# Order of softmax and splits in the pair units, forget gates moved to a value unit, gating and two token sums moved to GpSimd

## The chip, the cores and the metric

One NeuronCore of one Trainium2 chip. The kernel is one launch. Its time is the device time of the execution in microseconds, as the median of several runs. The engines are TensorE (PE in the rows, its weight loads PEld), VectorE (DVE), ScalarE (ACT), GpSimd (POOL) and SyncE (SP), which only issues DMAs here. Each engine runs its own list of instructions in order, and they wait for one another by semaphores. ScalarE and VectorE read the accumulators of TensorE (PSUM banks `acc` 0 to 3 and `side` 0 to 3); GpSimd works on SBUF alone.

## The reference

Two blocks on 512 tokens of 1024 features, all in float32. The first (gated pooling and a chunkwise linear recurrence) is over before the stretch that is touched. The second is a layer with four branches:

```python
def hybrid_layer(x, norm_g, w_in, ...):
    h = rms_norm_2(x, norm_g)
    (a_u, a_v, a_z, b_q, b_c, b_qi, b_ki, b_wi, b_z,
     c_b, c_c, c_x, c_z, d_q, d_k, d_v, d_f, d_z, gates) = split(h @ w_in)
    y_a = chunked_spatial_gating(a_u, a_v, ...) * silu(a_z)
    y_b = dsa_attention(b_q, b_c, b_qi, b_ki, b_wi, ...) * silu(b_z)
    y_c = short_gated_conv(c_b, c_c, c_x, conv_w) * silu(c_z)
    y_d = forgetting_attention(d_q, d_k, d_v, d_f, b_f) * silu(d_z)
    g = sigmoid(gates.reshape(b, s, 4, 1024))
    merged = sum_n g[n] * (y_n @ w_branch[n])
    return x + merged @ w_out

def forgetting_attention(q, k, v, f_logit, b_f):      # 4 heads of 128
    cum = cumsum(log_sigmoid(f_logit + b_f), axis=1)
    logits = q k^T / sqrt(128) + cum_q - cum_k        # causal
    return softmax(logits) v
```

## The kernel before

**Units.** The weights stream through as units of 128x1024 (some narrower), in the order `USED`. Each matrix product runs as three products of float32r parts: the weight is split into an upper part `w_hi` on ScalarE (`split_hi`, L713) and a lower part `w_lo` on VectorE (`split_lo`, L1308), and the tokens lie as `hT_hi` and `hT_lo`. Splits run ahead of their use. SyncE fetches the strips into a ring of five, GpSimd issues the DMAs that add up weights in DRAM for the pairs.

**The stretch.** After the units of branches a and c come four value units `dv` 0 to 3 (512 tokens, four accumulator banks, copied out to `fox_v` when `dv` 3 is done: two tiles by ScalarE, two by VectorE), then eight pairs `pa`, `pb`, `pd`, `pc` (p = 0 to 7), then `ga` 0, `ga` 1, `br` 0, `ga` 2, `ga` 3, `br` 1, and from there pairs of gates with `sa`, `sb`, `br`, `sc`, `sd`. A pair makes two panels (of q, k and the gates z of branches b and d) with seven instead of eight quarter products each (Strassen). For that, sums and differences of token quarters are made: tokens 1 and 2, 5 and 6 (`t_full` 5 and 6, for the `pc` units) and 4 and 3 (for `sc` and the third product of `br`). Each has an upper part `t_hi` (ScalarE) and a lower part `t_lo` (VectorE). The counter `t_step` follows the order in which they are made.

**A pair on the engines.** TensorE runs `pa` (one quarter product, twelve products of 128x256), `pb` (two), the slot of `pb`, `pd` (one), `pc`'s first product, the first of the next pair (`quad_first`), the slot of `pc`, `pc`'s second product. ScalarE copies four first parts (`keep_first` L927, L966, L974, L986), VectorE adds the others to them (L1699). A bank is free again when its part is copied or added. From pair 4 on the panels are gates: ScalarE makes exp, VectorE a bound, ScalarE ln and exp (together the sigmoid, `gate_sigmoid`), and VectorE multiplies it to z (`quad_finish`); for gates 0 to 3 it also multiplies the result with branch b's output (`y_tmp`, L1528), ScalarE makes the upper part (`end_upper`) and VectorE the lower part (`end_lower`).

**Slots.** The attention scores of branches b (scores 0 to 15) and d (16 to 31) run between the units, in slots of which each has its list of scores: 12 to 15 in the slots of `dv` and the one before, 16 to 31 two by two in the slots of `pb` and `pc` of pairs 4 to 7. A score is product, maximum (VectorE), exp (ScalarE), scale (VectorE), transpose (TensorE, next slot, L2312), copy `probsT` (ScalarE, L829), product with the values (slot after, L2327). The transposes share one bank (`side` 2): each waits for the copy of the one before (`bank2_read`). On ScalarE and VectorE a unit first works off its own part and its splits, then the slot.

**Forget gates.** In slot `FORGET_AT` = 34 (`pb` 1) TensorE transposes the logits, and VectorE and ScalarE make the cumulated log of the sigmoid in turns (L1672 to L1691, L915 to L918). `CUM_AT` = 36 turns it back.

**The end.** In `br` 0 VectorE makes the four products and lower parts of branch d (`end_tile`), then multiplies the result banks of `br` 0 with the sigmoids (L1972), which frees them for `br` 1. In `ga` 2 and `ga` 3 it makes tokens 3 and 4 (L1313 to L1315, L1342 to L1344, L1351). GpSimd has no arithmetic in the whole stretch: it parks `y` of branch a in DRAM at about 597 us, and fetches it back when `pc` 7 is done (819.5 us).

Of the kernel before, what the change touches and what calls it, by code (L numbers as in the profile page):

```python
# [46 lines left out]
for j in range(2 * KT):  # L47
# [12 lines left out]
                                               (5, "lo"), (6, "lo"), (3, "full"), (4, "full"), (4, "lo"), (3, "lo")])}  # L60
# [60 lines left out]
def to_split(k):  # L121

    if USED[k][0] in QUAD:
        return {"pa": [k + 3, k + 4], "pc": [k + 2, k + 3]}.get(USED[k][0], [])
# [66 lines left out]
FORGET_AT, CUM_AT = 34, 36  # L191
# [65 lines left out]
def program(nc, dram, out):  # L257
    f32, f32r, bf16, i32 = mybir.dt.float32, mybir.dt.float32r, mybir.dt.bfloat16, mybir.dt.int32
    ALU, ACT, AX = mybir.AluOpType, mybir.ActivationFunctionType, mybir.AxisListType
    with ExitStack() as ctx:  # L260
# [129 lines left out]
        forget = at("forget", M + 24576, [4, 2, S])  # L390
# [205 lines left out]
        def _(pool):  # L596
# [100 lines left out]
        def _(act):  # L697
# [254 lines left out]
            def quad_unit(k, kind, p):  # L952

                ends = p - QUADS // 2
                if kind == "pa":
# [16 lines left out]
                if kind == "pc":  # L972
# [3 lines left out]
                    for later_k in to_split(k):  # L976
                        split_hi(later_k)
# [3 lines left out]
            def quad_end(k, p):  # L981

                if p + 1 < QUADS:
                    keep_first(p + 1)
                act.wait_ge(unit_used, k + 1)
# [8 lines left out]
            for k, (kind, j) in enumerate(USED):  # L994
                if kind in QUAD:
                    quad_unit(k, kind, j)
                    if k in SLOT_AT:
                        side_slot(SLOT_AT[k])
                        act_forget(SLOT_AT[k])
                    if kind == "pc":  # L1000
                        quad_end(k, j)
# [153 lines left out]
                n = {("av", 1): 1, ("av", 2): 2, ("dv", 1): 5, ("dv", 2): 6}.get((kind, j))  # L1155
# [5 lines left out]
                if (kind, j) == ("ga", 3):  # L1161
# [54 lines left out]
        def _(dve):  # L1216
# [100 lines left out]
            def make_tokens(kind, j):  # L1317
# [12 lines left out]
                for n in {("av", 2): (1,), ("au", 2): (2,), ("dv", 2): (5, 6)}.get((kind, j), ()):  # L1330
                    dve.wait_ge(t_step, T_STEP[n if n > 2 else 2, "full"])
                    dve.wait_ge(t_hi_made, T_HI[n])
                    nc.vector.tensor_tensor(out=t_lo[n][:, :, :], in0=full[n], in1=t_hi[n][:, :, :].bitcast(f32),
                                            op=ALU.subtract).then_inc(t_step, 1)
                n = {("dv", 0): 5, ("ga", 2): 4}.get((kind, j))
                if (kind, j) == ("ga", 2):
                    difference(t3_full[:, :, :], t3_part[:, :, :], hi[1, 1], lo[1, 1], hi[0, 1], lo[0, 1])
                if n is not None:
                    dve.wait_ge(t_step, T_STEP[2, "lo"])
                    if n == 5:  # L1340
                        dve.wait_ge(parked, 32)
                    then(nc.vector.tensor_tensor(out=full[n], in0=hi[1, 0], in1=t_hi[2][:, :, :].bitcast(f32), op=ALU.add))  # L1342
                    then(nc.vector.tensor_tensor(out=rest[n], in0=lo[1, 0], in1=t_lo[2][:, :, :].bitcast(f32), op=ALU.add))
# [1328 lines left out]
```

## Time and profile before

| what | value |
| --- | --- |
| timed runs | 1129.44 us median of 3 (1127.44 to 1131.29) |
| profiled execution | 1130.89 us, span 1129.1 us, mean granted clock 0.994 |
| TensorE busy | 1101.7 us (98%) |
| VectorE busy | 744.8 us (66%) |
| ScalarE busy | 530.4 us (47%) |
| GpSimd busy | 74.4 us (7%) |
| `dv` 0 to the end of `dv` 3's slot | 665.8 to 696.5 us |
| pairs | 696.5 to 819.1 us |
| `ga` 0 to `sd` 2 | 819.1 to 877.2 us |

Times in rows are microseconds from the start of the span. A row of a timeline is start, length, engine, line, operation, what is written from what, and, in brackets, how long the engine had been idle before it and what ended that. The granted clock is a share of full speed: 1.00 is 2.4 GHz, 0.50 is 1.2 GHz.

### The profile page before, as it was taken

Reading aid. Unit: us, or ns where it says so; the run is one execution under the profiler, and the core shown is the slowest. Engines: PE = TensorE matmul, PEld = TensorE weight load, DVE = VectorE, ACT = ScalarE, POOL = GpSimd, SP = SyncE. Lnnn points to the kernel's source line nnn. Section 1 sums busy time; section 2 is a strip of 40 time slices with the busy share of each in tenths; the row PEclk is TensorE's granted clock in tenths of the full one; section 3 lists DMA queues with packets and bytes.
Section 4 is the critical chain, followed back from the end, with each engine's and each line's share of the span. In section 5 each row is a group of like instructions: output and inputs, shape, how many; then the busy total and the mean of one; then the engine's idle time right before and its main releaser. Section 6 shows DMA issues by size and latency. Waiting matters only on the chain.

```text
span 1129.1 us, 18866 instructions
## 1 busy us (share of the span) xinstructions
PE 1101.7 (98%) x7632; PEld 945.6 (84%) x7632; DVE 744.8 (66%) x1195; ACT 530.4 (47%) x897; POOL 74.4 (7%) x110
## 2 busy tenths in 40 slices
PE   9999999999999999999999999898898999999997
PEld 8888888788888888877888878897787999999986
DVE  6875776854785246478789886667738655556653
ACT  7562353324674325534442343456663444344543
POOL 1010101111110101011110000000000000000000
PEclk9999999999999999999999999899999999999999
DMA  9688878978778724368777222453333545455541
GB/s 370 217 274 250 205 204 260 246 201 218 191 150 212 249 92 165 134 171 221 167 208 205 72 84 83 124 166 103 101 135 92 166 138 162 140 161 167 143 167 75
DMA packets 61302, 194.56 MB, mean 172 GB/s; under 512 B 5648, under 2 KB 5648, under 8 KB 60704
## 3 DMA queue, kind: packets, MB, share of 16 engines
q1 hardware_dynamic: 39824, 127.19, 33.5%
q0 software_dynamic: 21248, 66.13, 24.7%
q8 instruction: 61, 1.00, 0.3%
q14 instruction: 25, 0.20, 0.1%
q10 hardware_dynamic: 144, 0.03, 0.0%
HBM read 187.04 MB, written 58.20 MB: 217 GB/s over the span
## 4 chain that ended last, share of the span: by engine, by line
PE 45%; DVE 5%; ACT 3%; issue 2%; ACTq 0%; DVEq 0%
PE acc L2045 6%; PE acc L2047 6%; PE acc L2046 6%; PE acc L2053 4%; PE acc L2055 4%; PE acc L2057 4%; PE side L2053 2%; PE side L2057 2%; PE side L2055 2%; PE side L2046 2%; PE side L2045 2%; PE side L2047 2%; PE side L2327 1%; PE side L2343 1%; PE side L2312 1%
## 5 line engine op out<-in xcount | busy, mean ns | idle before, releaser
L1308 DVE TENSOR_TENSOR w_lo<-raw,w_hi 128x1024 fp32r<-128x1024 f32 (+2 forms) x224 | 257.3, 1154 | 191.3 <-ACT w_hi L713 189.9
L713 ACT ACTIVATE w_hi<-raw 128x1024 fp32r<-128x1024 f32 (+2 forms) x224 | 222.3, 998 | 122.5 <-PE acc L2047 80.1
L2045 PE MATMUL acc<-hT_hi,w_hi 128*128 128x512 f32 x520 | 207.2, 398 | 0.0
L2047 PE MATMUL acc<-hT_hi,w_lo 128*128 128x512 f32 x520 | 202.8, 390 | 0.0
L2046 PE MATMUL acc<-hT_lo,w_hi 128*128 128x512 f32 x520 | 202.6, 390 | 0.0
L2045 PEld LDWEIGHTS acc<-hT_hi,w_hi 128*128 128x128 f32 x520 | 97.7, 188 | 21.2 <-issue 1.6
L2047 PEld LDWEIGHTS acc<-hT_hi,w_lo 128*128 128x128 f32 x520 | 97.6, 188 | 20.8
L2046 PEld LDWEIGHTS acc<-hT_lo,w_hi 128*128 128x128 f32 x520 | 97.8, 188 | 18.9
L2053 PE MATMUL acc<-t_hi,w_hi 128*128 128x256 f32 x212 | 61.8, 291 | 3.9 <-ACT fox_q L974 3.9
L2045 PE MATMUL acc<-w_hi,hT_hi 128*128 128x512 f32 (+1 forms) x152 | 61.1, 402 | 1.3 <-DVE y_tmp L1469 0.8
L2055 PE MATMUL acc<-t_lo,w_hi 128*128 128x256 f32 x212 | 61.1, 288 | 0.0
L2057 PE MATMUL acc<-t_hi,w_lo 128*128 128x256 f32 x212 | 61.0, 288 | 0.0
L2053 PE MATMUL acc<-hT_hi,w_hi 128*128 128x256 f32 x208 | 60.0, 288 | 0.0
L2057 PE MATMUL acc<-hT_hi,w_lo 128*128 128x256 f32 x208 | 59.3, 285 | 0.0
L2055 PE MATMUL acc<-hT_lo,w_hi 128*128 128x256 f32 x208 | 59.3, 285 | 0.0
L2047 PE MATMUL acc<-w_hi,hT_lo 128*128 128x512 f32 (+1 forms) x152 | 58.8, 387 | 0.0
L2046 PE MATMUL acc<-w_lo,hT_hi 128*128 128x512 f32 (+1 forms) x152 | 58.7, 386 | 0.0
L2053 PEld LDWEIGHTS acc<-t_hi,w_hi 128*128 128x128 f32 x212 | 42.0, 198 | 4.4 <-ACT fox_q L974 4.1
L2055 PEld LDWEIGHTS acc<-t_lo,w_hi 128*128 128x128 f32 x212 | 41.9, 198 | 0.3
L2057 PEld LDWEIGHTS acc<-t_hi,w_lo 128*128 128x128 f32 x212 | 41.8, 197 | 0.0
L2053 PEld LDWEIGHTS acc<-hT_hi,w_hi 128*128 128x128 f32 x208 | 40.4, 194 | 0.3
L2055 PEld LDWEIGHTS acc<-hT_lo,w_hi 128*128 128x128 f32 x208 | 40.4, 194 | 0.3
(484 smaller groups left out, 2343.3 us busy)
## 6 DMA issues: line engine op xcount, KB each, us to landing
raw<-sums_kept SPq DMA_DIRECT2D x44, 512.0 KB, 3.6
sums_kept<-in_st POOLq DMA_DIRECT2D x11, 1536.0 KB
sums_kept<-in_st POOLq DMA_DIRECT2D x11, 1024.0 KB
sums_kept<-in_st POOLq DMA_DIRECT2D x22, 512.0 KB
sums_kept<-sums_kept POOLq DMA_DIRECT2D x22, 512.0 KB
raw<-in_st SPq DMA_DIRECT2D x22, 512.0 KB, 3.9
ada_raw<-in_ada SPq DMA_DIRECT2D x16, 512.0 KB, 11.5
raw<-in_wo SPq DMA_DIRECT2D x16, 512.0 KB, 5.7
```

The costliest lines, as they stand in the source:

```text
L713: nc.scalar.activation(split_at(k)[0][:, 0:WIDTH.get(kind, U)], strip_of(k), ACT.Copy).then_inc(hi_made, 1)
L1308: nc.vector.tensor_tensor(out=lo[:, 0:width], in0=strip_of(k), in1=hi[:, 0:width].bitcast(f32), op=ALU.subtract).then_inc(lo_made, 1)
L2045: nc.tensor.matmul(ps, w[0], x[0], start=first, stop=False)
L2046: nc.tensor.matmul(ps, w[0], x[1], start=False, stop=False)
L2047: return nc.tensor.matmul(ps, w[1], x[0], start=False, stop=last)
L2053: nc.tensor.matmul(out_, w[0][:, cols], x[0][:, kt, :], start=first and kt == 0, stop=False, skip_group_check=not first)
L2055: nc.tensor.matmul(out_, w[0][:, cols], x[1][:, kt, :], start=False, stop=False, skip_group_check=not first)
L2057: ins = nc.tensor.matmul(out_, w[1][:, cols], x[0][:, kt, :], start=False, stop=kt == 3, skip_group_check=not first)
L2312: ins = nc.tensor.transpose(side[2][:, b * P:(b + 1) * P], probs[:, s % 2, b * P:(b + 1) * P], ident[:, :])
L2327: ins = nc.tensor.matmul(side[3][:, h * P:(h + 1) * P], v, probsT[:, s % 2, b * P:(b + 1) * P], start=(b == 0), stop=(b == blocks - 1))
L2343: nc.tensor.matmul(ps[:, 0:w], lat_q[:, h, tok], latT[:, 0:w], start=True, stop=False)
```

## The change

It changes the order in ScalarE's and VectorE's pair units, the slots of the forget gates, and which engine does the gating of the pairs and tokens 3 to 6. The arithmetic is the same, but token sums 4 and 5 negate in an instruction of their own.

- Splits: one per unit (`split_hi(k + AHEAD)`, `split_lo(k + AHEAD)`, `AHEAD` = 3) instead of two in `pa` and two in `pc`.
- ScalarE, `pb`: copy, split, slot, then the exp of the gate. `pd`: split, then the sigmoid. `pc`: copy, slot directly behind it, then `quad_end` (first copy of the next pair, split, last copy, exp), then `end_upper`. `pa`: sigmoid, split, `end_upper`.
- Forget gates in slot 30 (`dv` 2) instead of 34; turned back in slot 32 (`pb` 0); `pick`, which lies where an earlier tile is read until then, is made apart in slot 34. `forget` lies elsewhere.
- GpSimd: tokens 5 and 6 behind the parking DMAs, all of `quad_finish`, tokens 4 and 3.

```diff
-FORGET_AT, CUM_AT = 34, 36
+FORGET_AT, CUM_AT, PICK_AT = 30, 32, 34
@@ gpsimd
+            def fourth_tokens(n):
+                full, rest = t_full[n][:, :, :], t_rest[n][:, :, :]
+                then(nc.gpsimd.tensor_tensor(out=rest, in0=lo[1, 0], in1=t_lo[2]..., op=ALU.add))
+                then(nc.gpsimd.tensor_tensor(out=full, in0=hi[1, 0], in1=t_hi[2]..., op=ALU.add))
+                then(nc.gpsimd.tensor_tensor(out=full, in0=full, in1=rest, op=ALU.add))
+                nc.gpsimd.tensor_scalar(full, full, -1.0, None, ALU.mult).then_inc(t_step, 1)
+            def third_tokens(full, rest):
+                then(nc.gpsimd.tensor_tensor(out=rest, in0=lo[1, 1], in1=lo[0, 1], op=ALU.subtract))
+                then(nc.gpsimd.tensor_tensor(out=full, in0=hi[1, 1], in1=hi[0, 1], op=ALU.subtract))
+                nc.gpsimd.tensor_tensor(out=full, in0=full, in1=rest, op=ALU.add).then_inc(t_step, 1)
+            pool.wait_ge(parked, 32)
+            pool.wait_ge(t_step, T_STEP[2, "lo"])
+            fourth_tokens(5)
+            third_tokens(t_full[6][:, :, :], t_rest[6][:, :, :])
+            def quad_finish(n):
+                pool.wait_ge(silu_sig, QUAD_GATE0 + n + 1)
+                if n < 4:
+                    done_before = FINAL.index(("b", n))
+                    pool.wait_ge(y_made, done_before)
+                    nc.gpsimd.tensor_tensor(out=y_tmp[:, :], in0=z_d[:, n, :], in1=silu_e2[:, :], op=ALU.mult)\
+                        .then_inc(quad_gated, 1)
+                    pool.wait_ge(quad_gated, n + 1)
+                    nc.gpsimd.tensor_tensor(out=y_tmp[:, :], in0=y_tmp[:, :], in1=y_raw["b"][:, n, :], op=ALU.mult)\
+                        .then_inc(y_final, 1)
+                    pool.wait_ge(y_final, done_before + 1)
+                    pool.wait_ge(y_hi_made, done_before + 1)
+                    nc.gpsimd.tensor_tensor(out=y_lo["b"][:, n, :], in0=y_tmp[:, :], in1=y_hi["b"]..., op=ALU.subtract)\
+                        .then_inc(y_made, 1)
+                else:
+                    nc.gpsimd.tensor_tensor(out=z_d[:, n % 4, :], in0=z_d[:, n % 4, :], in1=silu_e2[:, :], op=ALU.mult)\
+                        .then_inc(quad_gated, 1)
+            for n in range(QUADS - 2):
+                quad_finish(n)
             pool.wait_ge(unit_used, STEP["pc", QUADS - 1] + 1)
             (fetch branch a back)
+            for n in (QUADS - 2, QUADS - 1):
+                quad_finish(n)
+            pool.wait_ge(summed, 2 * SPARSE)
+            fourth_tokens(4)
+            pool.wait_ge(y_made, 4 * TT)
+            third_tokens(t3_full[:, :, :], t3_part[:, :, :])
@@ scalar, quad_unit
                 if kind == "pb":
                     (copy L966)
+                    split_hi(k + AHEAD)
+                    side_slot(SLOT_AT[k])
+                    act_forget(SLOT_AT[k])
                     if ends >= 1:
                         quad_exp(2 * ends - 1)
-                if kind == "pd" and ends >= 1:
-                    gate_sigmoid(QUAD_GATE0 + 2 * ends - 1)
+                if kind == "pd":
+                    split_hi(k + AHEAD)
+                    if ends >= 1:
+                        gate_sigmoid(QUAD_GATE0 + 2 * ends - 1)
                 if kind == "pc":
                     (copy L974)
-                    for later_k in to_split(k):
-                        split_hi(later_k)
+                    side_slot(SLOT_AT[k])
+                    act_forget(SLOT_AT[k])
+                    quad_end(k, p)
                     if ends in (1, 2):
                         end_upper()
@@ vector, quad_unit
                 if kind == "pa":
                     if ends >= 1:
                         bound_gate(QUAD_GATE0 + 2 * ends - 2)
-                        quad_finish(2 * ends - 2)
-                    (two splits, end_lower)
+                    split_lo(k + AHEAD)
+                    if p == 0:
+                        lower_tokens(6)
...
                 if kind == "pb":
                     dve.wait_ge(part_kept, 4 * p + 2)
                     quad_add(p, 0, 1, 2)
+                    split_lo(k + AHEAD)
+                    side_slot(SLOT_AT[k])
+                    dve_forget(SLOT_AT[k])
```

ScalarE makes the upper parts of tokens 5 and 6 in `dv` 0 and `dv` 1 (before: `dv` 1 and `dv` 2), VectorE the lower parts in `dv` 1 and `pa` 0 (before: both in `dv` 2). The upper parts of tokens 4 and 3 and both lower parts are made in `br` 1 (before: three of them in `ga` 3). VectorE's four products of branch d wait for all eight gate products (`quad_gated`).

## Rows read from the trace of the kernel before

**Rows 1.** The page, busy time: engine, us, share of the span, instructions.

```profile
PE 1101.7 (98%) x7632; PEld 945.6 (84%) x7632; DVE 744.8 (66%) x1195; ACT 530.4 (47%) x897; POOL 74.4 (7%) x110
```

**Rows 2.** Waits from 680 to 880 us: us in total, times, longest.

```profile
PE side L2312 <- ACT probsT L829: 8.2, 6, 2.3
```

**Rows 3.** Timeline of TensorE, rows behind long gaps.

```profile
723.02 0.58 PE L2053 MATMUL acc<-t_hi,w_hi 128*128 128x256 f32 x1 [3.93 <-ACT fox_q L974]
...
767.28 0.30 PE L2312 MATMUL side<-ident,probs 128*128 128x128 f32 x1 [1.64 <-ACT probsT L829]
...
776.18 0.41 PE L2312 MATMUL side<-ident,probs 128*128 128x128 f32 x2 [2.32 <-ACT probsT L829]
...
786.82 0.41 PE L2312 MATMUL side<-ident,probs 128*128 128x128 f32 x2 [0.47 <-ACT probsT L829]
...
861.86 0.41 PE L2053 MATMUL side<-t_hi,w_hi 128*128 128x256 f32 x1 [2.43 <-DVE w_lo L1308]
```

**Rows 4.** Windows: busy us (instructions) of each engine, PEclk, DMA share, GB/s.

```profile
720.00:730.00 10.00, 6.98 (x36) 6.98 (x37) 6.96 (x11) 5.01 (x8) 0.00 (x0) 0.66 0.26 77
775.00:785.00 10.00, 8.82 (x60) 8.46 (x61) 6.85 (x18) 7.14 (x15) 0.00 (x0) 0.83 0.25 80
860.00:870.00 10.00, 7.59 (x36) 6.38 (x36) 9.24 (x11) 6.02 (x8) 0.00 (x0) 0.83 0.37 107
```

**Rows 5.** Timelines around `dv` 3 and of the forget gates.

```profile
689.61 0.58 PE L2045 MATMUL acc<-w_hi,hT_hi 128*128 128x512 f32 x1
...
691.73 0.49 DVE L1604 TENSOR_SCALAR probs<-probs,small 128x512 f32<-128x512 f32 x1
...
692.87 1.07 ACT L772 ACTIVATE fox_v<-acc 128x512 f32<-128x512 f32 x2
...
696.51 0.36 PE L2053 MATMUL acc<-hT_hi,w_hi 128*128 128x256 f32 x1
...
715.62 0.48 DVE L1673 MEMSET forget_r<- 128x512 f32 x1
...
722.08 0.63 ACT L918 ACTIVATE forget_r<-forget 4x512 fp32r<-4x512 f32 x1 [2.71 <-DVE forget L1684]
```

**Rows 6.** Timelines of GpSimd, and of VectorE beside it.

```profile
1.25 0.29 POOL L606 TENSOR_SCALAR_AFFINE_SELECT ident<-ident 128x128 f32<-128x128 f32 x1 [0.24 <-POOL ident L605]
...
212.92 2.13 POOL L650 MEMSET attn<- 128x2048 f32 x1
213.90 1.43 DVE L1465 TENSOR_SCALAR silu_e<-silu_e 128x512 f32<-128x512 f32 x1
...
454.69 0.63 POOL L671 TENSOR_SCALAR_AFFINE_SELECT mixT<-mixT 128x512 f32<-128x512 f32 x1 [11.21 <-DMA mixT<-in_w_s]
...
479.81 1.23 DVE L1308 TENSOR_TENSOR w_lo<-raw,w_hi 128x1024 fp32r<-128x1024 f32 x1
479.83 1.36 POOL L676 TENSOR_SCALAR_AFFINE_SELECT score<-score 128x128 f32<-128x128 f32 x1 [7.22 <-DVE score L1902]
```

**Rows 7.** Timelines of ScalarE and TensorE in pair 5.

```profile
763.14 0.63 ACT L860 ACTIVATE silu_e<-silu_e 128x512 f32<-128x512 f32 x1
763.68 1.99 ACT L713 ACTIVATE w_hi<-raw 128x1024 fp32r<-128x1024 f32 x2
...
764.52 0.27 PE L2312 MATMUL side<-ident,probs 128*128 128x128 f32 x1
...
766.88 0.26 ACT L829 ACTIVATE probsT<-side 128x128 f32<-128x128 f32 x1
```

**Rows 8.** Timelines of ScalarE, VectorE and TensorE around `br` 0.

```profile
836.20 0.63 ACT L860 ACTIVATE silu_e<-silu_e 128x512 f32<-128x512 f32 x1
...
841.35 0.69 DVE L1528 TENSOR_TENSOR y_tmp<-z_d,yd_raw 128x512 f32<-128x512 f32 x1
...
849.97 0.68 DVE L1972 TENSOR_TENSOR m_full<-acc,sig 128x512 f32<-128x512 f32 x1
...
850.95 0.39 PE L2045 MATMUL acc<-yc_hi,w_hi 128*128 128x512 f32 x1
```

More of the change, by code:

```diff
@@ L389, in program @@
         fox_v = at("fox_v", R_MP + 8192, [P, TT, S])
-        forget = at("forget", M + 24576, [4, 2, S])
+        forget = at("forget", R_0, [4, 2, S])
         forget_r = at("forget_r", R_GP, [P, S], f32r)
@@ L683, in _ @@
                 pool.dma_start(ya_kept[:, 2048 * n:2048 * n + 2048], ya[n]).then_inc(parked, 16)
+            hi = {(r, c): quarter(hT_hi, r, c).bitcast(f32) for r in (0, 1) for c in (0, 1)}
+            lo = {(r, c): quarter(hT_lo, r, c).bitcast(f32) for r in (0, 1) for c in (0, 1)}
+            def fourth_tokens(n):
+                full, rest = t_full[n][:, :, :], t_rest[n][:, :, :]
+                then(nc.gpsimd.tensor_tensor(out=rest, in0=lo[1, 0], in1=t_lo[2][:, :, :].bitcast(f32), op=ALU.add))
+                then(nc.gpsimd.tensor_tensor(out=full, in0=hi[1, 0], in1=t_hi[2][:, :, :].bitcast(f32), op=ALU.add))
+                then(nc.gpsimd.tensor_tensor(out=full, in0=full, in1=rest, op=ALU.add))
+                nc.gpsimd.tensor_scalar(full, full, -1.0, None, ALU.mult).then_inc(t_step, 1)
@@ L984, in quad_end @@
                     keep_first(p + 1)
+                split_hi(k + AHEAD)
                 act.wait_ge(unit_used, k + 1)
@@ L1329, in make_tokens @@
                     nc.vector.tensor_tensor(out=full[2], in0=full[2], in1=lo[1, 1], op=ALU.subtract).then_inc(t_step, 1)
[L1330 to L1337, printed above, removed]
-                if n is not None:
[L1339 to L1343, printed above, removed]
-                    nc.vector.scalar_tensor_tensor(out=full[n], in0=full[n], scalar=-1.0, in1=rest[n],
-                                                   op0=ALU.mult, op1=ALU.subtract).then_inc(t_step, 1)
-                if (kind, j) == ("dv", 1):
-                    difference(full[6], rest[6], hi[1, 1], lo[1, 1], hi[0, 1], lo[0, 1])
-                if (kind, j) == ("ga", 3):
-                    dve.wait_ge(t_step, T_STEP[4, "full"])
-                    dve.wait_ge(t_hi_made, T_HI[4])
-                    nc.vector.tensor_tensor(out=t_lo[4][:, :, :], in0=full[4], in1=t_hi[4][:, :, :].bitcast(f32),
-                                            op=ALU.subtract).then_inc(t_step, 1)
+                n = {("av", 2): 1, ("au", 2): 2, ("dv", 1): 5}.get((kind, j))
+                if n is not None:
+                    lower_tokens(n)
+                if (kind, j) == ("br", 1):
+                    lower_tokens(4)
                 if (kind, j) == ("br", 1):
@@ L1721, in quad_unit @@
                         bound_gate(QUAD_GATE0 + 2 * ends - 2)
-                        quad_finish(2 * ends - 2)
-                    for later_k in to_split(k):
-                        split_lo(later_k)
-                    if ends in (1, 2):
-                        end_lower()
+                    split_lo(k + AHEAD)
+                    if p == 0:
+                        lower_tokens(6)
                     dve.wait_ge(part_kept, 4 * p + 1)
@@ L1741, in quad_unit @@
                     quad_add(p, 1, 1, 2)
-                    if ends >= 1:
-                        quad_finish(2 * ends - 1)
-                    for later_k in to_split(k):
-                        split_lo(later_k)
-                    if ends in (1, 2):
-                        end_lower()
+                    side_slot(SLOT_AT[k])
+                    dve_forget(SLOT_AT[k])
+                    split_lo(k + AHEAD)
             gates = 0
@@ L1789, in _ @@
                     dve.wait_ge(bank3_read, 2 * TT)
+                    dve.wait_ge(quad_gated, QUADS)
+                    finals[0] += 4
                     for h in range(4):
```

50 lines of the change are left out of this document (17 added, 33 removed).

## The prediction

> **What bounds the kernel now.** I read the page's busy shares first, then TensorE's waits and its own rows in the stretch that the change touches, then the granted clock there, and last the queues of the engines that it waits for. TensorE is busy for 98% of the span [rows 1], so nearly every other place is paid by its products and only its gaps can be given back. Their waits lie mostly between 660 and 880 us: six waits of the transposes in the pair units for ScalarE's copy `probsT`, 8.2 us in all [rows 2], and the long single ones of [rows 3]. A gap also costs after it has ended: the granted clock falls to its lower level (1.2 GHz) behind three of them [rows 4]. A mean of 0.66 over 10 us is 0.34 x 10 / 0.5 = 6.8 us at half clock, of which 1 us lies before TensorE goes on: 2.9 us lost behind the gap of 3.9 us. A mean of 0.83 is 3.4 us at half clock, 1.7 us lost, behind the gaps of 2.3 and of 2.4 us.
>
> That makes three losses. A, the forget gates in pair 1: 3.9 + 2.9 = 6.8 us. B, the softmax of pairs 4 to 7: 8.2 + 1.7 = 9.9 us. C, the combined tokens 3 and 4: TensorE idle for 0.6 us before 860 (861.86 - 2.43 = 859.43 [rows 3]) and 2.4 of the ten us behind it [rows 4], + 1.7 = 4.7 us. Together 21.4 us; this change can win no more.
>
> **A: the forget gates move from `pb` 1 to `dv` 2.** The chain is VectorE from L1673 to the scan, then ScalarE's `forget_r` copy: 715.62 to 722.71, 7.1 us, in which ScalarE stands in its queue waiting for VectorE [rows 5]. Moved, it starts when the softmax of score 15 has left VectorE. In the same slot that was 2.6 us behind the start of `dv` 3's products (691.73 + 0.49 against 689.61) [rows 5]; the four transposes that now precede `dv` 3 make it 2.2 us. TensorE goes through `dv` 3 and its slot in 696.51 - 689.61 = 6.9 us. ScalarE is free at 2.2 + 7.1 = 9.3 us, but behind the forget copy stand the narrow split of `pd` 0 (half of the 0.95 us of a wide one [rows 7], 0.5) and the copy of value tile 0 (0.5 [rows 5]). Only the latter frees the bank that `quad_first(0)` wants: 10.3 us. So the gap of 3.9 us doesn't go, it becomes one of 10.3 - 6.9 = 3.4 us, with the same half clock behind it (1.7 to 2.9). I take -0.5 us for A; between -1.7 and 0. What covered the copies of the value tiles before was that nothing stood in front of them. VectorE loses the tokens 5 and 6 there (six instructions of 1.2 us, and one lower part that goes to `pa` 0); it had no TensorE wait behind it, so 0. On GpSimd they run from about 605 us, where its queue had only the two parking DMAs, and have 70 us.
>
> **B: pairs 4 to 7.** In a `pc` unit the copy of `probs` used to stand behind two splits and, in pairs 5 and 6, an upper copy. Now it stands directly behind L974, which is done long before TensorE reaches the slot: of the 8.2 us, 1.6 and 0.5 lie in the `pb` slots of pairs 5 and 6 [rows 3] and 6.1 in `pc` slots, of which 0.3 stand in pair 4, ahead of all this, and 5.8 go. In pair 7's `pb` one split now stands before it and not behind, which I price at 0 to 0.7, and take 0.7; for pair 4 I leave 0.5.
>
> In a `pb` unit it is the other way about, because `end_upper` of `pa` now waits for GpSimd. Pair 5, on the clock of the trace [rows 7]: the sigmoid's last step ends at 763.77, now 0.6 us later for the split of `pd` 5 that stands before it, 764.4; `pb` 5 ends on TensorE at 764.5. On VectorE two such products took 0.7 us each (as L1528 in [rows 8]) and could pass in the shadow of ScalarE's two splits. On GpSimd no row shows a two-input product. The nearest is the select of 128x512 with one input, 0.63 us [rows 6]; two inputs read one after the other make 1.26 us, an estimate, and the one that I take. Ends: 0.63 (the second input free) and 1.9 (three times, the output too). Over 128x1024: 2.4 us, 1.2 to 3.8. A hand-over on GpSimd took 0.24 us [rows 6]; I take 0.2. So `y_final` comes at 764.4 + 2 x 1.46 = 767.3; then on ScalarE the upper copy 0.5, L966 0.3 (as short as L829 in [rows 7]), the split of `pa` 6 0.95, `probsT` 0.3 and the hand-over 0.1: 769.5. TensorE has nothing left before the second transpose at 765.6 (767.28 - 1.64 [rows 3]). Gap 3.9 us instead of 1.6.
>
> The Trainium skill (GPSIMD Engine Reference, 3.1 Elementwise) puts the two-input operation at about twice VectorE's time, 4.5 us for 2048 columns; for 512 that would be some 1.2 us by estimate, and the gap would be the same. No row here shows it.
>
> On top comes the port. A select of 128 columns took 1.36 us when a VectorE subtraction of two tiles had begun just before it, and ended 0.15 us behind it; and a VectorE step that takes 0.4 us took 1.43 us while a GpSimd memset ran [rows 6]. So one waits out the whole instruction of the other. In pair 5 VectorE's split of `pc` 5 falls between the two products: +1.0 us, gap 4.9. In pair 6 the same chain stands against `pb` 6, but TensorE comes there later by the half clock behind the first gap (2.9 us, of which ScalarE's chain shares some part): between 2.0 and 4.9 us; I take 3.0, instead of 0.5. Half clock: 2.9 behind the first (longer than the 3.9 of the trace), 1.7 behind the second. After: 4.9 + 3.0 + 0.5 + 0.7 + 4.6 = 13.7 us, against 9.9: +3.8.
>
> What the page SBUF (State Buffer) of the Trainium skill says under "Who interferes with whom" is that rule: a VectorE instruction with two SBUF inputs and a GpSimd one that reads SBUF exclude each other for a whole instruction. Its rule speaks against this change; without it B would be +2.8. The rows of the select and the memset agree, neither with a two-input GpSimd operation.
>
> **C: tokens 3 and 4.** They leave VectorE (six instructions over 128x1024, 1.2 us each as L1308 in [rows 6]) and with them go the late splits and the 4.7 us. What is late next is the bank of `br` 0: four products of branch d and their lower parts, from 841.35 on, then L1972, whose end at 849.97 + 0.68 = 850.65 came 0.3 us before `br` 1 began at 850.95 [rows 8]. Token 4 now runs on GpSimd just then: the last gate's sigmoid ended at 836.83 [rows 8] and the gate product takes 1.5, so from 838.3 three times 2.4 + 0.2 and one of 1.2 fill the time to 847.3. Each of VectorE's eight two-input steps that meets one waits; three meet one, each for half of it, 1.2 us: 3.6 - 0.3 cushion = 3.3 us of gap at `br` 1, and 2.3 us of half clock (between 1.7 and 2.9). 5.6 against 4.7: +0.9. Ends: all 4.7 won if nothing waits, +6 if every instruction of token 4 is waited out. Token 3 follows when the finals are done and has TensorE's `br` 1 and `sa`, 8 us, for three times 2.6: fits, just.
>
> **Sum.** -0.5 + 3.8 + 0.9 = +4.2 us. The profiled execution took 1130.9 us (span 1129.1), the median of the timed runs is 1129.4; the difference of 1.5 lies inside their spread, and I put the sum on the median, taking off a half us for gaps that overlap: 1133.
>
> **Rivals.**
> 1. The port isn't shared this way and the products take 1.26 us. For it: the GpSimd rows that show a wait are a select and a memset, no product. Against: both rows wait to the end of the other. A -0.5, B +2.8, C -4.7: -2.4 us, 1127.0. Not slower.
> 2. GpSimd is fast (0.63 and 1.2 us). For it: the select's row as it stands. Against: a product reads twice as much. Then the gaps of pairs 5 and 6 are 3.9 - 1.3 = 2.6 and 1.7, B is 2.6 + 1.7 + 1.2 + 1.7 = 7.2, -2.7, C -4.7, A -1.2: -8.6 us, 1120.8.
> 3. GpSimd is slow (1.9 and 3.8 us). The gaps of pairs 5 and 6 grow by two products each, 2 x 0.64: 2.6 us. Token 4 fills 5 us more and meets two more steps of VectorE, each for some 2 us: 4. 4.2 + 2.6 + 4 = +11, 1140. It decides as soon as a product is over 1.5 us.
> 4. The forget gates do what the title says, and A's 6.8 us go: this would need the copy of the value tile ahead of the gates in ScalarE's queue, and it stands behind them. Little speaks for it; 5 us less on any of the others.
>
> **How the numbers follow.** The forecast (exclusive port, 1.26 us) has 45%, with a range of its own of 1128 to 1138. Rival 3 has 7%, rival 1 20%, rival 2 with what is left and rival 4 28%. What a measurement of this kernel can tell from no change is 0.3%, 3.4 us, so 1126.0 to 1132.8 is "same". Of the 45%, 33 lie above and 12 within; of rival 1, 13 within and 7 below; of rivals 2 and 4, 26 below and 2 within. Slower 40%, same 27%, faster 33%. Eight in ten: 1121 to 1140, which leaves out parts of rivals 2 and 3.
>
> **What would show it.** Right: at the end of `dv` 3's slot TensorE waits some 3.4 us for ScalarE's copy of `fox_v`, and none in `pc` 1; GpSimd's 512-column products show about 1.3 us; TensorE waits 3 to 5 us for `probsT` in the `pb` slots of pairs 5 and 6 and hardly in `pc` slots; the idle time before ScalarE's `yb_hi` is a wait for GpSimd; VectorE steps with two inputs show twice their length beside GpSimd's; `br` 1 waits for L1972. Wrong: no wait at `quad_first(0)`; a clock that stays at 2.4 GHz through pairs 5 and 6; `yb_hi` that waits for nothing; `br` 1 without a gap, which would take the forecast to rival 1.

## The result and the profile after

The changed kernel took **1143.22 us** in the median (1142.01 to 1143.43, 4 runs), the kernel before 1128.74 us beside it: ratio 1.0123, 95% interval 1.0103 to 1.0143. That is 14.5 us slower; the forecast was 4 us slower, and the value lies outside its range. The profiled execution took 1143.43 us, its span 1141.6 us.

The page's busy shares of the kernel after, to be held against [rows 1]: GpSimd has gained 61 us, TensorE 4 us (instructions that run at half clock are longer; the mean granted clock is 0.985, before 0.994).

```profile
PE 1105.9 (97%) x7632; PEld 948.8 (83%) x7632; DVE 741.1 (65%) x1167; ACT 529.8 (46%) x897; POOL 135.7 (12%) x140
```

TensorE's own rows after a gap, from its timeline in the kernel after (start, length, operation, idle time before it and what ended that):

```profile
618.71 0.55 PE L2332 MATMUL side<-ident,probs 128*128 128x128 f32 x3 [1.45 <-DVE probs L1640]
632.18 0.90 PE L2332 MATMUL side<-ident,probs 128*128 128x128 f32 x3 [6.66 <-DVE probs L1640]
679.20 0.50 PE L2065 MATMUL acc<-w_hi,hT_hi 128*128 128x512 f32 x1 [0.77 <-DVE y_tmp L1505]
708.72 0.55 PE L2073 MATMUL acc<-hT_hi,w_hi 128*128 128x256 f32 x1 [3.28 <-ACT fox_v L818]
778.05 0.45 PE L2332 MATMUL side<-ident,probs 128*128 128x128 f32 x1 [4.71 <-ACT probsT L875]
799.01 0.41 PE L2332 MATMUL side<-ident,probs 128*128 128x128 f32 x2 [3.56 <-ACT probsT L875]
865.75 0.77 PE L2065 MATMUL acc<-yc_hi,w_hi 128*128 128x512 f32 x1 [4.16 <-DVE m_full L1992]
```

The last four are the gaps of the forecast (A; B in pairs 5 and 6; C). The first two are not in it: they lie where tokens 5 and 6 run on GpSimd, for which the forecast put down 0. The row at 679.20 also stands in the kernel before, at 671.00, 8.2 us earlier, while the first wait for `probs` both have stands at 517.40 in after and at 519.04 in before, 1.6 us later: 9.8 us are lost between the two places. From 671.00 on, the span of before has 458.1 us left, after has 462.4 from 679.20: 4.3 us more, which is the size of the whole forecast. These differences are of the two profiled executions, whose spans are 12.5 us apart (-1.6 + 9.8 + 4.3); the medians are 14.5 us apart.

GpSimd, then VectorE, in that stretch of the kernel after, from their timelines:

```profile
610.20 2.38 POOL L688 TENSOR_TENSOR t_rest<-hT_lo,t_lo 128x1024 f32<-128x1024 f32 x1 [13.96 <-DMA ya_kept<-ya_lo]
612.66 3.26 POOL L689 TENSOR_TENSOR t_full<-hT_hi,t_hi 128x1024 f32<-128x1024 f32 x1
616.00 2.43 POOL L690 TENSOR_TENSOR t_full<-t_full,t_rest 128x1024 f32<-128x1024 f32 x1
618.52 2.79 POOL L691 TENSOR_SCALAR t_full<-t_full 128x1024 f32<-128x1024 f32 x1
621.31 2.38 POOL L695 TENSOR_TENSOR t_rest<-hT_lo 128x1024 f32<-128x1024 f32 x1
623.77 3.23 POOL L696 TENSOR_TENSOR t_full<-hT_hi 128x1024 f32<-128x1024 f32 x1
627.08 2.67 POOL L697 TENSOR_TENSOR t_full<-t_full,t_rest 128x1024 f32<-128x1024 f32 x1
```

```profile
610.32 3.35 DVE L1355 TENSOR_TENSOR w_lo<-raw,w_hi 128x1024 fp32r<-128x1024 f32 x1
613.59 2.61 DVE L1501 TENSOR_SCALAR silu_e<-silu_e 128x512 f32<-128x512 f32 x1
...
617.61 1.04 DVE L1640 TENSOR_SCALAR probs<-probs,small 128x384 f32<-128x384 f32 x1
...
621.59 3.19 DVE L1355 TENSOR_TENSOR w_lo<-raw,w_hi 128x1024 fp32r<-128x1024 f32 x1
624.70 0.68 DVE L1505 TENSOR_TENSOR y_tmp<-acc,silu_e 128x512 f32<-128x512 f32 x1
625.41 2.13 DVE L1564 TENSOR_TENSOR y_tmp<-y_tmp,yc_raw 128x512 f32<-128x512 f32 x1
628.32 1.98 DVE L1572 TENSOR_TENSOR yc_lo<-y_tmp,yc_hi 128x512 fp32r<-128x512 f32 x1 [0.77 <-ACT yc_hi L1089]
```

A split takes 1.23 us elsewhere [rows 6], here 3.35 and 3.19. Each begins 0.1 to 0.3 us behind the start of a GpSimd addition and ends 1.1 us, about its own length, behind that addition's end. The six stretched instructions take 14.3 us together; the same six took 4.7 us in the kernel before (1.23, 0.43, 0.42, 1.23, 0.69 and 0.69), 9.6 us less. The product at 624.70, which has one input in an accumulator, keeps its 0.68 us. VectorE has no such time to spare here: it is busy for 18.3 of the 20 us from 600 on in the kernel before. The windows of the kernel after (us; busy time and count of PE, PEld, DVE, ACT, POOL; granted clock; DMA):

```profile
600.00:620.00 20.00, 18.55 (x83) 14.66 (x82) 18.57 (x28) 5.49 (x8) 9.55 (x4) 1.00 0.53 193
620.00:640.00 20.00, 13.34 (x55) 10.52 (x54) 17.34 (x25) 5.22 (x10) 9.60 (x4) 0.83 0.16 52
```

The granted clock of 0.83 over 20 us is 0.17 x 20 / 0.5 = 6.8 us at 1.2 GHz, partly inside the idle time.

### The profile page after: what moved, and what is told of

It reads as the page before. It is cut to its first block and busy times, and to the rows that moved or that the text cites. A ratio compares the mean times of both kernels' runs of the same rounds, so it can differ in the third digit from the quotient of the medians.

```text
span 1141.6 us, 18863 instructions
## 1 busy us (share of the span) xinstructions
PE 1105.9 (97%) x7632; PEld 948.8 (83%) x7632; DVE 741.1 (65%) x1167; ACT 529.8 (46%) x897; POOL 135.7 (12%) x140
## 5 line engine op out<-in xcount | busy, mean ns | idle before, releaser
L1355 DVE TENSOR_TENSOR w_lo<-raw,w_hi 128x1024 fp32r<-128x1024 f32 (+2 forms) x224 | 267.6, 1197 | 207.7 <-ACT w_hi L759 206.1
L2067 PEld LDWEIGHTS acc<-hT_hi,w_lo 128*128 128x128 f32 x520 | 97.6, 188 | 20.9
L2077 PEld LDWEIGHTS acc<-hT_hi,w_lo 128*128 128x128 f32 x208 | 41.9, 202 | 0.0
```

Of the source, the lines that this page charges most:

```text
L1355: nc.vector.tensor_tensor(out=lo[:, 0:width], in0=strip_of(k), in1=hi[:, 0:width].bitcast(f32), op=ALU.subtract).then_inc(lo_made, 1)
L2067: return nc.tensor.matmul(ps, w[1], x[0], start=False, stop=last)
L2077: ins = nc.tensor.matmul(out_, w[1][:, cols], x[0][:, kt, :], start=False, stop=kt == 3, skip_group_check=not first)
```

## The experiments

All times are medians; a ratio is to the kernel before, with its 95% interval. Names starting with `b_` are the kernel before with one thing more or other, the rest start from the kernel after.

### Tokens 5 and 6: the unpriced step

**t56_dve** and **b_pool56** move the same work each way.

```diff
 # t56_dve (from after): GpSimd's fourth_tokens(5), third_tokens(6) deleted; VectorE:
+if (kind, j) == ("dv", 0): (full[5] as in before)
+if (kind, j) == ("dv", 1): difference(full[6], rest[6], ...)
 # b_pool56 (from before): those two deleted on VectorE, and on GpSimd behind the parking DMAs:
+fourth_tokens(5); third_tokens(t_full[6][:, :, :], t_rest[6][:, :, :])
```

> The kernel after, with tokens 5 and 6 made on VectorE again (5 in dv 0, 6 in dv 1), all else as after. Theory: the 10 us by which after exceeds the forecast come from GpSimd's seven instructions over 128x1024 between 610 and 630 us, which keep VectorE's splits and products waiting; without them 1133 to 1134 us, no TensorE wait between 610 and 650, and the same gaps as after at the first pair (3.3), in pb of pairs 5 and 6 (4.7, 3.6) and at br 1 (4.2). Rival, the loss lies in the unit order elsewhere (splits one per unit, softmax ahead of them) and the tokens only mark the place: still 1140 or more.

> The kernel before, with only tokens 5 and 6 moved to GpSimd, behind the parking DMAs as in after. Theory: two TensorE waits for probs between 615 and 635, together 8 us, and half clock behind them: +9 to +10.5 us, 1138 to 1140. Rival, the tokens alone fit into VectorE's slack and only collide with something else of the change: 1129 to 1131.

Measured: t56_dve 1136.04 us (1.0057, 1.0040 to 1.0074), 7.2 us less than after; b_pool56 1137.37 us (1.0078, 1.0054 to 1.0102), 7.8 us more than before. Neither gives the full 10. In t56_dve the waits at 618 and 632 are gone, but the one at the first pair is 5.67 us and no longer 3.28: the tokens on VectorE make the forget gates start later (2.6 us before the end of `dv` 3's slot, in after 5.0 us before it), so taking them off VectorE was worth 2.4 us there, which the forecast had put at 0 as well. In b_pool56 TensorE's waits in the stretch are 2.3, 0.7 and 1.2 us, not 8. GpSimd's seven instructions begin 3.2 us later there, at 613.43, so the split at 611.41 and the step behind it are over by then; the later splits take 2.87 and 2.84 us. Its profiled execution took 1134.95 us, 2.4 us less than the median, so these rows do not show all of the 7.8 us.

**t56_late** keeps them on GpSimd and starts them when `cz` 3 is done.

```diff
+pool.wait_ge(unit_used, STEP["cz", 3] + 1)
 fourth_tokens(5)
-# ScalarE, upper parts: ("dv", 0): 5, ("dv", 1): 6   VectorE, lower part: ("dv", 1): 5
+# ScalarE, upper parts: ("dv", 1): 5, ("dv", 3): 6   VectorE, lower part: ("dv", 3): 5
```

> The kernel after, with tokens 5 and 6 still on GpSimd, the same seven instructions, but started when cz 3 is done (about 667 us) and not at 610; their upper parts are made on ScalarE in dv 1 and dv 3, the lower parts on VectorE in dv 3 and pa 0. VectorE has its last top-k round behind it there. Theory, the place decides, since VectorE is busy for 18.5 of 20 us at 610 to 630 and for 8 of 20 us from 680 on: VectorE's operations are as long as beside any GpSimd work, yet TensorE doesn't wait: 1133 to 1135. Rival, the operation costs wherever it stands: 1138 or more, with TensorE waits for probs or w_lo in dv 0 to dv 2.

Measured: 1139.56 us (1.0089, 1.0072 to 1.0106), 3.7 us less than after, 3.5 us more than t56_dve: the rival's number, by another wait than it named. One wait takes the place of two: 4.58 us and not 0.77 for the result of `cz` 3 (`y_tmp`, VectorE), because three steps of VectorE ahead of it took 2.62, 0.89 and 3.36 us beside GpSimd's additions (`silu_e`, `probs` and a split; 0.43, 0.49 and 1.23 us when free). A better place helps, but GpSimd still met a VectorE instruction with a due time.

### What on GpSimd holds VectorE up

Extra work at the place of tokens 5 and 6 in the kernel before, over 128x1024: 17 memsets (**b_memset**), a memset and seven multiplications by -1 (**b_onein**), a memset and seven additions of a tile to itself (**b_twoin**).

```diff
+for _ in range(16): nc.gpsimd.memset(t_rest[5][:, :, :], 0.0)                         # b_memset, and one more
+for _ in range(6): nc.gpsimd.tensor_scalar(t, t, -1.0, None, ALU.mult)                # b_onein, and one more
+for _ in range(6): nc.gpsimd.tensor_tensor(out=t, in0=t, in1=t, op=ALU.add)           # b_twoin, and one more
```

> The kernel before, with 17 GpSimd memsets of 128x1024 at the place where after makes tokens 5 and 6 (extra work, nothing else changed). They write and read nothing. Theory one, VectorE's operations with two SBUF inputs wait for a GpSimd instruction that reads: the splits (1.22 us) and the products (0.69) keep their length, at most the one-input steps (0.43) show up to 1.5 us; 1129 to 1131. Theory two, any GpSimd instruction holds the port against any VectorE instruction: splits of 2.3 us, and several us lost on TensorE, 1134 to 1139.

> The kernel before, with a memset and seven GpSimd multiplications by -1 over 128x1024 (one SBUF input, extra work) at the place of tokens 5 and 6. If one input costs half of two, each takes about 1.2 us, the stretch is over in 10 us, and VectorE's splits that meet one take up to 2.4 us: 1130 to 1133. If GpSimd's time goes by elements written, each takes 2.4 to 2.8 us as in after, for 18 us, splits take up to 3.5 us: 1134 to 1138. That it reads is what matters, not how many inputs: in both cases VectorE's two-input operations wait, as they did not beside the memsets.

> The kernel before, with a memset and seven GpSimd additions over 128x1024 with two SBUF inputs (extra work) at the place of tokens 5 and 6; b_onein had the same with one input, 18 us long, and there VectorE's splits kept their 1.2 us. Theory, only GpSimd's two-input form keeps VectorE's splits and products waiting: splits of 2.4 to 3.6 us, TensorE waits of several us for probs, 1135 to 1140. Rival, it was the tokens' tiles or their chance timing: splits of 1.2 us, 1130 to 1133.

Measured: 1130.83 us (1.0010, 1.0000 to 1.0019), 1132.90 (1.0024, 1.0013 to 1.0035) and 1132.40 (1.0036, 1.0022 to 1.0050). The medians hardly tell the second and third apart; the rows do. GpSimd and VectorE in b_memset, in b_onein and in b_twoin:

```profile
612.24 16.48 POOL L688 MEMSET t_rest<- 128x1024 f32 x16 [12.18 <-DMA ya_kept<-ya_lo]
613.37 1.11 DVE L1471 TENSOR_SCALAR silu_e<-silu_e 128x512 f32<-128x512 f32 x1
619.54 1.23 DVE L1313 TENSOR_TENSOR w_lo<-raw,w_hi 128x1024 fp32r<-128x1024 f32 x1
```

```profile
612.74 17.89 POOL L689 TENSOR_SCALAR t_rest<-t_rest 128x1024 f32<-128x1024 f32 x6
617.87 1.23 DVE L1314 TENSOR_TENSOR w_lo<-raw,w_hi 128x1024 fp32r<-128x1024 f32 x1
619.73 0.81 DVE L1535 TENSOR_TENSOR y_tmp<-y_tmp,yc_raw 128x512 f32<-128x512 f32 x1
```

```profile
613.30 13.36 POOL L689 TENSOR_TENSOR t_rest<-t_rest 128x1024 f32<-128x1024 f32 x6
618.45 1.86 DVE L1314 TENSOR_TENSOR w_lo<-raw,w_hi 128x1024 fp32r<-128x1024 f32 x1
620.95 1.67 DVE L1535 TENSOR_TENSOR y_tmp<-y_tmp,yc_raw 128x512 f32<-128x512 f32 x1
```

Beside memsets the split keeps its 1.23 us and only one-input steps grow, from 0.43 to 1.11 and from 0.42 to 0.84. Beside one-input multiplications, which do read, the split keeps its time too, and the product takes 0.81 us (free: 0.69). Beside two-input additions they take 1.86 and 1.67 us. The kernel after has one more product that began while a multiplication ran, and that one did not run free. GpSimd's row, then VectorE's:

```profile
857.27 3.10 POOL L691 TENSOR_SCALAR t_full<-t_full 128x1024 f32<-128x1024 f32 x1
857.76 1.41 DVE L1564 TENSOR_TENSOR y_tmp<-z_d,yd_raw 128x512 f32<-128x512 f32 x1
```

It took 0.7 us more than its 0.69, and still ended 1.2 us before the multiplication, so it did not wait that instruction out. The other way round GpSimd waits: in b_pool56 a multiplication that began while a split was running took 3.63 us, against 2.77 us for the last one in b_onein. So it is GpSimd's two-input form that holds VectorE's two-input operations up for microseconds; that it reads costs them between nothing and 0.7 us. The Trainium skill (SBUF — State Buffer, Who interferes with whom) has it that they contend with a GpSimd instruction that reads SBUF and not with one that only writes; the memsets bear out the second half, the multiplications bear out the first only in small part. The expectation of b_onein, that VectorE's two-input operations wait in either case, was wrong. The time of b_twoin is its rival's (1130 to 1133), the rows are its theory's: an addition of a tile to itself took 2.2 us (13.36 / 6) with the waits between, not 2.4 to 3.3, and fewer of VectorE's steps met one. Why b_onein's median is 3.5 us above before stays open: its profiled execution took 1129.4 us and the nine others 1130.6 to 1133.5, so the rows are those of the one execution that lost nothing.

### The forecast's losses A, B and C, one by one

These start from t56_dve (1136.04). **d_qf**: `quad_finish` and its lower parts on VectorE as in before. **d_fgt**: the forget gates' last two steps one slot later. **d_t34**: tokens 3 and 4 on VectorE as in before. **d_all**: all three; of the change there is left one split per unit, the softmax behind the copies and the earlier forget gates.

```diff
 # d_qf
-pc: side_slot(...); split_lo(k + AHEAD)
+pc: side_slot(...); quad_finish(2 * ends - 1); split_lo(k + AHEAD); end_lower()
 # d_fgt: the wait for fgt_sum, ScalarE's forget_r copy and VectorE's two steps behind it
-in slot FORGET_AT = 30
+in slot FORGET_END = 31
 # d_t34
-fourth_tokens(4); third_tokens(t3_full, t3_part)      # GpSimd
+("ga", 2): difference(t3_full, ...), full[4]; ("ga", 3): lower_tokens(4)    # VectorE
```

> Tokens 5 and 6 on VectorE (as t56_dve, 1136.0) and quad_finish with the lower parts on VectorE too, at the places of the kernel before; the softmax stays directly behind the copies. Theory of the prediction for B: the gaps in pb of pairs 5 and 6 (4.9 and 3.6 us) are the GpSimd products; with 0.7 us instead of 1.3 to 2.1 each, some 2.5 us go from each gap and with the clock behind them 1.5 to 3 more: 1127.5 to 1129.5. Rival, the gaps come from ScalarE's own order (sigmoid, split, upper copy ahead of probsT), and the engine of the products doesn't matter: 1134.5 to 1136.

> As t56_dve, and the forget gates in two parts: up to the scan in slot 30 as in after, the two last steps (ScalarE's forget_r copy, VectorE's correction) in slot 31, behind the copies of the value tiles. Theory of the prediction for A: quad_first(0) waits because ScalarE stands in the forget gates' queue until the scan ends; it is now free 3.3 us earlier, so the gap of 5.7 us falls to about 2.4 and 1 to 2 us of half clock go too: 1131 to 1132. Rival, VectorE's copies of the other two value tiles, which also stand behind the chain, take over: the gap moves on to a product of pa 0, 1134.5 to 1136.

> As t56_dve, and tokens 3 and 4 on VectorE as in the kernel before. Theory of the prediction for C: the 4.2 us gap at br 1 is VectorE's finals waiting for GpSimd's token 4; it goes, and the old one of 2.4 us with its 0.8 us beside it, for the late splits behind VectorE's tokens, comes back; both with about 2 us of half clock: 1134 to 1136. Rival, branch d's finals are late by themselves (they start later relative to br 0 than before): the gap at br 1 stays over 3 us and the old one is added, 1139.

> All three together: GpSimd has no arithmetic left, what remains of the change is the softmax directly behind the copies, one split per unit, and the forget gates in two parts in dv 2 and dv 3. Theory, the three add up: 1136.0 - 4 - 7.5 - 0.5 = 1124, 1122 to 1126, below the kernel before. Rival, VectorE as the only engine is now the one that is late and the gains overlap: 1128 to 1130.

Measured: d_qf 1133.75 us (1.0038, 1.0022 to 1.0054), d_fgt 1132.37 (1.0028, 1.0015 to 1.0040), d_t34 1134.78 (1.0044, 1.0029 to 1.0059), d_all 1129.48 (0.9997, 0.9986 to 1.0007). A's theory holds: the gap falls from 5.67 to 2.33 us. C's too: 4.15 us at `br` 1 go, 2.43, 1.37 and 0.49 us come back. B's does not: 2.3 us won where 6.5 to 8.5 were expected, 0.75 us from the rival's range. The wait in `pb` 5 falls from 4.87 to 2.61 us, in `pb` 6 it stays (3.55 and 3.78), and `pb` 7 gets one of 2.27, so the three together are as long as before (8.4 and 8.7 us). TensorE begins `ga` 0 at 820.94 instead of 821.79, only 0.85 us earlier; the rest of the gain comes at `br` 1, whose wait falls from 4.15 to 2.73 us. d_all went as its rival said (1128 to 1130); it beats t56_dve by 6.6 us, where the three single edits make 7.2. ScalarE in d_all shows what holds the softmax up, ahead of the `probsT` that TensorE waits for at 784.6 in `pb` 6:

```profile
780.77 1.04 ACT L730 ACTIVATE w_hi<-raw 128x1024 fp32r<-128x1024 f32 x1
782.35 0.63 ACT L966 ACTIVATE yb_hi<-y_tmp 128x512 fp32r<-128x512 f32 x1 [0.54 <-DVE y_tmp L1550]
782.89 0.36 ACT L982 ACTIVATE z_d<-acc 128x256 f32<-128x256 f32 x1
783.15 1.05 ACT L730 ACTIVATE w_hi<-raw 128x1024 fp32r<-128x1024 f32 x1
784.10 0.37 ACT L846 ACTIVATE probsT<-side 128x256 f32<-128x256 f32 x1
```

Two splits and an upper copy stand ahead of the copy with the due time. That led to three edits of d_all. **x_b** puts the slot of `pb` directly behind its copy, on both engines, and `end_upper` and `end_lower` of `pa` behind that slot; in `pc`, VectorE makes the gate's product ahead of the slot and the one with branch b's output behind it. **x_a** has the forget gates in slots 28 and 29. **x_c** makes token 4 before token 3. **x_all** has all three.

```diff
 # x_b, ScalarE in pb
-split_hi(k + AHEAD); side_slot(...); act_forget(...)
+side_slot(...); act_forget(...); split_hi(k + AHEAD); end_upper()      # end_upper no longer in pa
 # x_b, VectorE in pb likewise (end_lower no longer in pa), and in pc
-side_slot(...); dve_forget(...); quad_finish(2 * ends - 1)
+quad_gate(2 * ends - 1); side_slot(...); dve_forget(...); quad_product(2 * ends - 1)
 # x_a
-FORGET_AT, FORGET_END = 30, 31
+FORGET_AT, FORGET_END = 28, 29
 # x_c, VectorE
-("ga", 2): token 3, token 4;  ("ga", 3): lower part of 4
+("ga", 2): token 4;  ("ga", 3): lower part of 4, token 3      # ScalarE: upper copy of 3 in br 1
```

> As d_all (1129.5; all arithmetic on VectorE), with the pb unit put in the order that the pc unit has: on ScalarE the slot stands directly behind the copy, ahead of the split and of the upper copy of the gated product, which moves from pa to behind the slot of pb; VectorE likewise, and in pc only the gate's own product stands ahead of its slot. In d_all TensorE waits 2.6, 3.8 and 2.3 us in the pb slots of pairs 5, 6 and 7 for probsT, and ScalarE works without a break there (two splits and an upper copy ahead of it, 2.7 us). Theory, the order on ScalarE is what is left of loss B, whoever makes the products: these gaps go to under 1 us each, 1121 to 1124. Rival, ScalarE is simply full in pairs 4 to 7: the splits that move behind the slot are late for the next units, the gaps move to w_lo, 1127 to 1130.

> As d_all, with the forget gates two slots earlier (part one in dv 0, part two in dv 1), so that nothing of them stands before the copies of the value tiles. Theory of the prediction for A: the gap of 2.4 us at quad_first(0) and the half clock behind it (granted clock 0.86 over 10 us, 1.4 us) are the chain of the forget gates in ScalarE's queue; both go: 1125.5 to 1126.5. Rival, VectorE is too full in dv 0 and dv 1 (tokens 5 and 6, the gates, the last product of branch c) and TensorE waits there for probs instead: 1128 to 1130.

> As d_all, with token 4 (needed first, by sb) made in ga 2 and token 3 in ga 3 behind the split and the lower part of token 4, and the upper copy of token 3 in br 1. Theory, the gaps of 2.4, 1.4 and 0.5 us after 858 in d_all are 7.3 us of token work in one piece ahead of a split that sb needs; spread out it fits: 1125 to 1126. Rival, VectorE's work from branch d's finals on is too much however it is ordered: the gap moves to the pair's last unit, 1128 to 1130.

> The three together. Theory, all three losses of the kernel before go: 1129.5 - 3.5 - 6.5 - 4 = 1115.5, 1114 to 1119. Rival, they share slack and only half adds up: 1121 to 1124.

Measured: x_b 1126.44 us (0.9954, 0.9938 to 0.9971), the first that beats the kernel before; x_a 1132.88 (1.0027, 1.0015 to 1.0040), x_c 1131.37 (1.0011, 1.0000 to 1.0021), x_all 1130.45 (0.9996, 0.9984 to 1.0007). x_b closes the waits for `probsT` in `pb` 5 to 7 but the splits behind the slot are late by 1.1, 1.4 and 1.6 us, and a wait of 1.51 us for `probsT` appears in pair 7's `pc`, each theory being half right. x_b changes both queues, so ScalarE's and VectorE's shares are not separated. x_a and x_c go the way their rivals said, and are slower than these put them (1128 to 1130). x_all missed both of its ranges: the gaps of x_a and x_c stand in it side by side (4.03 and 4.53 us) and take back what x_b gains. TensorE's rows behind the new gaps, in x_a and in x_c:

```profile
690.64 1.00 PE L2339 MATMUL side<-ident,probs 128*128 128x128 f32 x4 [4.03 <-DVE probs L1626]
```

```profile
866.21 0.58 PE L2081 MATMUL side<-t_hi,w_hi 128*128 128x256 f32 x1 [4.61 <-ACT gate_a L1190]
```

From x_b on, **y_a** moves the upper copies of tokens 5 and 6 to `dv` 1 and `dv` 3, since this row of ScalarE in x_b, with a split and a softmax queued behind it, showed what the forget gates still waited for:

```profile
690.32 1.06 ACT L1176 ACTIVATE t_hi<-t_full 128x1024 fp32r<-128x1024 f32 x1 [4.41 <-DVE t_full L1333]
```

**y_c** and **z_all** try two more orders of tokens 3 and 4, **y_all** is y_a with y_c, **z_all** includes y_a.

```diff
 # y_a
-ScalarE, upper parts: ("dv", 0): 5, ("dv", 1): 6;  VectorE, lower part: ("dv", 1): 5
+ScalarE, upper parts: ("dv", 1): 5, ("dv", 3): 6;  VectorE, lower part: ("dv", 3): 5
 # y_c, VectorE
-("ga", 2): token 3, token 4;  ("ga", 3): lower part of 4;  ("br", 1): lower part of 3
+("ga", 2): token 3;  ("ga", 3): lower part of 3, token 4;  ("sa", 2): lower part of 4
 # z_all, VectorE: as y_c, but
+("br", 1), behind its products: token 4;  ("sb", 2): lower part of 4
```

> As x_b, with the upper copies of tokens 5 and 6 on ScalarE in dv 1 and dv 3 (not dv 0 and dv 1) and the lower part of token 5 in dv 3. In x_b ScalarE waits 4.4 us for token 6 in dv 1, so the split of dv 3 and with it the softmax in slot 29 and VectorE's start on the forget gates come 2 us late. Theory, the gap of 2.3 us at quad_first(0) is that delay: under 0.5 us left, and the half clock behind it goes: 1122.5 to 1124. Rival, something else in front of the value tiles' copies is as late: 1125.5 to 1127.

> As x_b, with token 3 in ga 2 and its lower part with token 4 in ga 3 behind the split, the upper copy of token 4 on ScalarE in sa behind gate_a's copy. (x_c put token 4 first and had ScalarE wait for token 3 ahead of gate_a's copy; a gap of 4.6 us.) Theory, sb of the first gate pair waits only for its split, which stands behind 7.3 us of tokens in one piece, and for gate_a; with 3.7 us in front it is ready: the 2.4 and 0.4 us after 857 go, 1122.5 to 1124. Rival, the pair's later units then wait for token 4: 1126 to 1128.

> As x_b (1126.4), with both of the next two edits. Theory, the losses at the first pair and at the end are queueing that can be undone: 1126.4 - 3 - 3.5 = 1120, 1118 to 1123. Rival, as in x_all the gains don't add: 1125 to 1128.

> As y_a (1122.4), with token 3 in ga 2, its lower part in ga 3, token 4 in br 1 behind the products of br 1's results (in y_all they stood behind token 4 and TensorE waited 4.1 us for them), and token 4's two parts in sb. Theory, loss C is queueing on VectorE in front of something that has a due time (the split of sb, gate_a's copy, the results of br 1), and with token 4 behind all three the gaps of 2.4 and 0.5 us and their 1.7 us of half clock go: 1117.5 to 1119.5. Rival, VectorE holds more work between 838 and 862 than TensorE leaves it, and the gap moves on again, to sc: 1121 to 1124.

Measured: y_a 1122.41 us (0.9938, 0.9920 to 0.9956), no gap at the first pair and no half clock there; y_c 1125.83 (0.9970, 0.9953 to 0.9987), no gain on x_b; y_all 1121.94 (0.9931, 0.9915 to 0.9948), no gain on y_a; z_all **1120.17** (0.9925, 0.9911 to 0.9939), 9.5 us faster than the kernel before. The gap of C has moved with every order: to 4.61 us (x_c), to 4.11 us at `br` 2 (y_c), and in z_all to `br` 2's second half. TensorE in z_all:

```profile
852.45 0.47 PE L2081 MATMUL acc<-ya_hi,w_hi 128*128 128x512 f32 x1 [0.47 <-DVE merged_part L2008]
857.87 0.58 PE L2089 MATMUL side<-hT_hi,w_hi 128*128 128x256 f32 x1 [2.42 <-DVE w_lo L1327]
```

Its VectorE is busy for 9.83 of the 10 us from 850 on. So between branch d's products and `br` 2 there is more work on VectorE than time, and z_all's rival has the mechanism: the late split is that of `sc`. The time lies between the two ranges. That z_all beats y_a is not shown: their intervals overlap, and their waits there are as long (2.9 us in both).

## Why the prediction was wrong, by its own steps

- **"It had no TensorE wait behind it, so 0. On GpSimd they run from about 605 us ... and have 70 us."** This is the step that failed: a term put at 0 that cost 7.2 us (t56_dve) to 7.8 us (b_pool56) of the 10 by which the result exceeds the forecast. With the 2.4 us that moving the tokens off VectorE gains at the first pair, t56_dve's 7.2 become about 9.6. The prediction asked when the tokens are due and not whom they meet. The prediction itself had the exclusive port and applied it to B and C; at 605 us it didn't look at VectorE, which in the kernel before is busy for 18.3 of 20 us there and hands `probs` to TensorE every 7 to 9 us. The memsets exclude mere presence of GpSimd.
- **The rule of the port.** It was right for GpSimd's additions, which no row of the prediction showed; that was in part luck. The memset's row had a one-input step of VectorE beside it, and says nothing of two-input ones, which ran free beside memsets (b_memset, 1.23 us).
- **The one-input multiplication, 1.2 us.** It took 2.79 and 3.10 us. The Trainium skill (GPSIMD Engine Reference, 3.1 Elementwise) gives two inputs twice VectorE's time: the additions' 2.4 us against 1.2 agree.
- **A, -0.5.** Forecast a gap of 3.4 us at `quad_first(0)`, measured 3.28, released by the copy named. d_fgt shows the mechanism. That VectorE's relief was worth nothing there was wrong by 2.4 us.
- **B, +3.8, the second step that was wrong, though its number held.** Gaps of 4.9, 3.0, 0.5 and 0.7 us forecast, 4.71, 3.56, 0.22 and 0.38 measured (`pb` 5, `pb` 6, pair 4, pair 7; the last in `pc` and not in `pb`). GpSimd's products of 512 columns took 1.27 to 1.30 us (1.26 forecast), the two that met VectorE's split 2.12. Taking GpSimd out (d_qf) closes pair 5's by half, leaves pair 6's and opens one of 2.27 us in pair 7: 0.85 us in all pairs together. So the engine of the products is a small part of B, and that B's sum agrees is in good part luck. What was left was the order of the queues (x_b). Whether that order would also close the gaps with the products on GpSimd was not tried.
- **C, +0.9.** Gap of 3.3 us forecast, 4.16 measured, at the place and by the releaser named. d_t34 puts C at 1.3 us. Three of VectorE's steps grew beside token 4, by 4.3 us together (2.88, 2.03 and 1.41 us for 0.69 each) where 3.6 were forecast.
- **The sum.** A, B and C made +4.2, and the part of the span behind 671 us grew by 4.3. With the 9.8 us before that it is 14.1, of which the profiled spans give back 1.6 ahead of all this. The measured time lies nearest to rival 3 (1140), but not for its reason: it wanted products of over 1.5 us, and they took 1.27 to 1.30.

## What to carry to other kernels

Work moved to an idle engine is priced by what runs beside it on the engine that shares its port: read that engine's rows at the time at which the moved work will run, not only its due time. The best version has no arithmetic on GpSimd: none of its 9.5 us came from a move between engines, and 7.1 of them (from d_all to y_a) came from the order in the queues of ScalarE and VectorE: behind each copy that frees a bank comes first what TensorE waits for next, and waits for another engine's result (an upper copy, a chain that returns) go behind that. When a gap moves with every order, as C's did, the engine has too much to do there, and reordering ends.

## What the runs showed of the hardware that was not expected

- GpSimd's multiplication of 128x1024 by a constant is no faster than its addition of two tiles: 2.77 us for the last one in b_onein, 2.38 us for the shortest additions in after.
- It hardly holds up VectorE's two-input operations (split 1.23 us as when free; products 0.69, 0.81 and once 1.41 us beside it, 0.69 free), GpSimd's additions do (split up to 3.35 us, product up to 2.88 us). It waits for them itself: 3.63 us when it began during a split (b_pool56).
- VectorE's one-input step of 128x512 in SBUF waits for both a memset (1.11 us) and an addition (2.61 us), and took 0.43 us free. Beside the multiplications of b_onein two such one-input steps grew (0.84 us for 0.42, 1.27 us for 0.48) and others did not.
